# Moving averages of a pooling mixer: running sums on GpSimd, or products with a band matrix on TensorE

## The reference, cut to what matters

```python
csum = pad(cumsum(u, axis=1))                 # per group g of 64 channels
lo   = max(t + 1 - w, 0); cnt = min(t + 1, w)
mean = (csum[:, 1:, g] - csum[:, lo, g]) / cnt
y    = mean - u                               # then y @ w_pool[g], times pool_scale
```

## Time and profile before

| | us |
|---|---|
| median of 3 runs | 1396.54 (1396.28 to 1396.85) |
| the profiled execution | 1395.26 |
| its span | 1393.5 |
| TensorE busy (share of the span) | 1308.9 (94%) |
| VectorE | 727.0 (52%) |
| GpSimd | 562.0 (40%) |
| ScalarE | 476.4 (34%) |

### The profile page before, as it was taken

The page is one execution under the profiler, slowest core; times in us unless marked ns, Lnnn a source line. Parts: engine busy times, 40 slices in busy tenths (PEclk is TensorE's granted clock), DMA queues, the critical chain, the costliest instruction groups (busy, mean ns, idle before and its releaser), DMA issues.

```text
span 1393.5 us, 16477 instructions
## 1 busy us (share of the span) xinstructions
PE 1308.9 (94%) x6506; PEld 1025.5 (74%) x6506; DVE 727.0 (52%) x1045; ACT 476.4 (34%) x948; POOL 562.0 (40%) x312
## 2 busy tenths in 40 slices
PE   7999789997999999999899988989989999999996
PEld 5887555576888888888778855556868888888885
DVE  3154787725876153361464366877169650633506
ACT  4323556822322122221132334577222221312211
POOL 3541840023544444444444429200326444444444
PEclk9999778999999999999989986699989999999998
DMA  7531100022243323232144320000314332333311
GB/s 232 149 91 46 47 1 1 1 81 71 77 135 103 94 92 105 91 104 93 46 128 114 98 60 2 0 1 2 106 46 134 101 98 92 105 91 101 96 61 61
DMA packets 66557, 109.99 MB, mean 79 GB/s; under 512 B 16880, under 2 KB 17200, under 8 KB 66352
## 3 DMA queue, kind: packets, MB, share of 16 engines
q1 hardware_dynamic: 65328, 104.73, 24.4%
q10 hardware_dynamic: 1152, 4.19, 1.0%
HBM read 106.82 MB, written 2.10 MB: 78 GB/s over the span
## 4 chain that ended last, share of the span: by engine, by line
PE 87%; DVE 8%; ACT 2%; POOL 1%; issue 1%; DMA 1%; SPq 0%; POOLq 0%; ACTq 0%; DVEq 0%
PE ps L606 16%; PE ps L607 15%; PE ps L608 15%; PE ps L603 8%; PE ps L605 8%; PE ps L604 8%; PE ps L653 4%; PE ps L661 3%; DVE probs_a L1223 2%; PE ps L697 2%; DVE negmax L1174 1%; PE ps L715 1%; PE ps L682 1%; POOL rstd L494 1%; PE ps L582 1%
## 5 line engine op out<-in xcount | busy, mean ns | idle before, releaser
L480 POOL TENSOR_TENSOR w_lo<-raw,w_hi 128x1024 fp32r<-128x1024 f32 x184 | 452.9, 2466 | 739.5 <-ACT w_hi L857 739.4
L857 ACT ACTIVATE w_hi<-raw 128x1024 fp32r<-128x1024 f32 x184 | 193.9, 1059 | 615.2 <-PE ps L608 398.0
L603 PE MATMUL ps<-xt_hi,w_lo 128*128 128x512 f32 x512 | 202.0, 395 | 4.8 <-DVE xt_lo L1068 4.8
L605 PE MATMUL ps<-xt_lo,w_hi 128*128 128x512 f32 x512 | 200.8, 392 | 0.0
L604 PE MATMUL ps<-xt_hi,w_hi 128*128 128x512 f32 x512 | 200.7, 392 | 0.0
L606 PE MATMUL ps<-w_hi,mt_lo 128*128 128x512 f32 x384 | 150.1, 391 | 0.0
L608 PE MATMUL ps<-w_lo,mt_hi 128*128 128x512 f32 x384 | 149.4, 389 | 0.0
L607 PE MATMUL ps<-w_hi,mt_hi 128*128 128x512 f32 x384 | 149.4, 389 | 0.0
L606 PE MATMUL ps<-w_hi,xt_lo 128*128 128x512 f32 x320 | 127.7, 399 | 4.5 <-DVE xt_lo L1068 3.7
L608 PE MATMUL ps<-w_lo,xt_hi 128*128 128x512 f32 x320 | 126.3, 395 | 0.0
L607 PE MATMUL ps<-w_hi,xt_hi 128*128 128x512 f32 x320 | 126.3, 395 | 0.0
(11 more groups left out here) (174 smaller groups left out, 1974.8 us busy)
## 6 DMA issues: line engine op xcount, KB each, us to landing
raw<-in_w_up SPq DMA_DIRECT2D x64, 512.0 KB, 3.7
raw<-in_w_down SPq DMA_DIRECT2D x64, 512.0 KB, 3.6
raw<-in_w_in SPq DMA_DIRECT2D x40, 512.0 KB, 3.7
raw<-in_w_out SPq DMA_DIRECT2D x8, 512.0 KB, 3.6
raw<-in_w_out SPq DMA_DIRECT2D x12, 256.0 KB, 3.8
xres<-in_x SPq DMA_DIRECT2D x4, 512.0 KB, 6.0
rows<-in_ln_g ACTq DMA_DIRECT2D x4, 512.0 KB, 4.1
rows<-in_ln_b ACTq DMA_DIRECT2D x4, 512.0 KB, 5.8
```

What stands on the lines that cost most here:

```text
L480: nc.gpsimd.tensor_tensor(w_lo[:, u % RING], raw[:, u % RING], w_hi[:, u % RING].bitcast(F32), ALU.subtract).then_inc(s_lo_ready, 1)
L603: mm(o, wl[:, c], a_hi[:, k, :], start=first, stop=False)
L605: return mm(o, wh[:, c], a_lo[:, k, :], start=False, stop=end)
L857: A(w_hi[:, u % RING], raw[:, u % RING], ACT.Copy).then_inc(s_hi_ready, 1)
```

## The change

The means are taken by products on the values as they lie in `proj_b`, tokens on the partitions. The output of `matmul(o, of, band)` is `of` transposed times `band`: the 128 tokens of a tile against a band of 144 columns (128 tokens of the same tile and 16 of the next), with 1/w inside the window and 1 subtracted at the token itself. So one step sums, divides, subtracts and turns. For the first tile the band's first 128 columns are another matrix, with the true counts. The products of the four tiles add up in bank 7, 64 channels of a group in each half of the partitions. GpSimd's sums, their buffers (`upad`, `boxb`, `boxc`), the table of 1/count and the semaphore `s_pool_y` go; the constants get the bands; `boxed` takes the result, and `cst` moves to the space behind it.

```diff
-SIDE = {0: ("turn", 6), 1: ("turn", 12), 2: ("turn", 7), 3: ("turn", 8), 4: ("turn", 9), ...
+SIDE = {0: ("turn", 6), 1: ("turn", 12), 2: ("box", 0), 3: ("box", 1), 4: ("turn", 9), ...
...
+    q = np.arange(BAND)                       # BAND = P + 16
+    for g, w in enumerate(WINDOWS):
+        inside = (q[None, :] >= p[:, None]) & (q[None, :] - p[:, None] < w)
+        here = q[None, :] == p[:, None]
+        k[:, K_BAND + g * BAND:K_BAND + (g + 1) * BAND] = inside / np.float32(w) - here
+        k[:, K_FIRST + g * P:K_FIRST + (g + 1) * P] = (inside / np.minimum(q + 1, w).astype(np.float32) - here)[:, 0:P]
...
-        cst = sb("cst", [4, TT * 6])
+        cst = at("cst", ra + 28672, [4, TT * 6])
...
-                pool.wait_ge(s_side_emptied, nth("side_emptied", layer, 4))
-                nc.gpsimd.memset(upad[:, :, 0:16], 0.0)
...
-                for c in range(2):
-                    b, u_ = boxb[:, c, :], upad[:, c, :]
-                    add = nc.gpsimd.tensor_tensor
-                    link(add(b[:, w], u_[:, w], u_[:, back(1)], ALU.add))
...
-                    add(b[:, w], b[:, w], u_[:, w], ALU.subtract).then_inc(s_pool_y, 1)
...
+                elif kind == "box":
+                    for tt in range(TT):
+                        for g in (2 * c, 2 * c + 1):
+                            r, u0 = 64 * (g % 2), T_U - T_VCM + 64 * g
+                            o, of = ps[r:r + 64, 7, :], proj_b[:, tt, u0:u0 + 64]
+                            band = kc[:, K_BAND + g * BAND:K_BAND + (g + 1) * BAND]
+                            if tt == 0:
+                                mm(o[:, 0:P], of, kc[:, K_FIRST + g * P:K_FIRST + (g + 1) * P], start=True, stop=False,
+                                   skip_group_check=True)
+                                last = mm(o[:, P:BAND], of, band[:, P:BAND], start=False, stop=False, skip_group_check=True)
+                            else:
+                                n = BAND if tt < TT - 1 else P
+                                last = mm(o[:, tt * P:tt * P + n], of, band[:, 0:n], start=False, stop=tt == TT - 1,
+                                          skip_group_check=True)
                 elif kind == "pool":
-                    pe.wait_ge(s_pool_y, nth("pool_y", layer, c + 1))
-                    last = mm(ps[:, 7, :], w_blk[:, c, :], boxb[:, c, 16:16 + SEQ], start=True, stop=True)
+                    last = mm(ps[:, 7, :], w_blk[:, c, :], boxed[:, c, :], start=True, stop=True)
...
-                        last = A(upad[:, c - Q_U, 16:16 + SEQ], b, ACT.Copy)
+                    elif kind == "box":
+                        last = A(boxed[:, c, :], b, ACT.Copy)
```

More of the change, by code:

```diff
@@ L66 @@
 TASKS = 2 * TASKS_A
-SIDE = {0: ("turn", 6), 1: ("turn", 12), 2: ("turn", 7), 3: ("turn", 8), 4: ("turn", 9), 5: ("compress", 0),
+SIDE = {0: ("turn", 6), 1: ("turn", 12), 2: ("box", 0), 3: ("box", 1), 4: ("turn", 9), 5: ("compress", 0),
         6: ("turn", 10), 7: ("turn", 11), 8: ("turn", 13), 9: ("turn", 14), 10: ("cmp_scores", 0),
@@ L78 @@
 R_CAQ, R_SAQ, R_CAK, R_SAK, R_CCK, R_SCK, R_CCQ, R_SCQ = 0, 16, 48, 64, 96, 128, 192, 224
-K_INV = K_ROPE + TT * ROPE_W
-K_CM = K_INV + 2 * SEQ
+BAND = P + 16
+K_BAND = K_ROPE + TT * ROPE_W
+K_FIRST = K_BAND + 4 * BAND
+K_CM = K_FIRST + 4 * P
 K_CB = K_CM + TT * 32
@@ L83 @@
 K_HALF = K_LAM + 2 * DEPTH
-K_ROWS = K_HALF + 1
-K_END = K_ROWS + 6
+K_END = K_HALF + 1
 K_MASK = K_END
@@ L105, in shape_constants @@
     rope = np.concatenate([ca * A_SCALE, sa * A_SCALE, ca, sa, cc, sc, cc * C_SCALE, sc * C_SCALE], -1)
-    k[:, K_ROPE:K_INV] = rope.reshape(P, -1)
-    tt = np.arange(SEQ)
-    for c in range(2):
-        for half in range(2):
-            cnt = np.minimum(tt + 1, WINDOWS[2 * c + half])
-            k[64 * half:64 * half + 64, K_INV + c * SEQ:K_INV + (c + 1) * SEQ] = 1.0 / cnt
+    k[:, K_ROPE:K_BAND] = rope.reshape(P, -1)
+    q = np.arange(BAND)
[4 more added lines that the diff above has]
+        k[:, K_FIRST + g * P:K_FIRST + (g + 1) * P] = (inside / np.minimum(q + 1, w).astype(np.float32) - here)[:, 0:P]
     n = np.arange(32)
@@ L120, in shape_constants @@
     k[:, K_HALF] = -0.5
-    k[:, K_ROWS:K_ROWS + 4] = (p[:, None] // 32 == np.arange(4))
-    k[:, K_ROWS + 4:K_ROWS + 6] = (p[:, None] // 64 == np.arange(2))
     return k
@@ L159 @@
     cmp_rows=1, cmp_max=1, cmp_shifted=1, cmp_factor=1, cmp_exp=1, cmp_probs=1,
-    pool_y=2, pool_hi=2, pool_mixed=2,
+    pool_hi=2, pool_mixed=2,
     scores=TASKS, negmax=TASKS, exped=TASKS, probs=TASKS, p_turned=TURNS, p_copied=TURNS,
@@ L201, in build @@
         xt_hi, xt_lo = at("xt_hi", ra, [KT, SEQ], F32R), at("xt_lo", ra + 16384, [KT, SEQ], F32R)
-        qkt, upad = at("qkt", ra, [S_N, SEQ]), at("upad", ra + 2048 * S_N, [2, 16 + SEQ])
-        boxc = at("boxc", ra + 28800, [16 + SEQ])
+        qkt, boxed = at("qkt", ra, [S_N, SEQ]), at("boxed", ra + 2048 * S_N, [2, SEQ])
         rb = room(32768)
@@ L209, in build @@
         probs_a, pt_a = at("probs_a", rb + 10368, [3, 2, SEQ]), at("pt_a", rb + 22656, [2, 2, SEQ])
-        boxb = at("boxb", rb + 3 * 2048, [2, 16 + SEQ])
         rc = room(32768)
@@ L320, in build @@
         s_value_weights = sem("value_weights")
-        s_pool_y = sem("pool_y")
         s_pool_hi = sem("pool_hi")
@@ L937, in side @@
                     n, (kind, c) = SIDE_NUMBER[t], SIDE[t]
-                    if kind not in ("turn", "compress", "cmp_turn"):
+                    if kind not in ("turn", "box", "compress", "cmp_turn"):
                         return
@@ L951, in side @@
                         last = A(cmp_pt[0:64, 2 * c:2 * c + 2, 1, :], src[0:64, :, 1, :], ACT.Copy)
-                    elif Q_U <= c < Q_QC:
-                        last = A(upad[:, c - Q_U, 16:16 + SEQ], b, ACT.Copy)
+                    elif kind == "box":
+                        last = A(boxed[:, c, :], b, ACT.Copy)
                     else:
```

## The result

The changed kernel takes 1373.72 us (median of 4 runs, 1371.85 to 1376.60) where the kernel before took 1396.41 in the same measurement (1394.55 to 1396.85): a ratio of 0.9842, interval 0.9819 to 0.9865. In four later sets of runs, each on one chip, the kernel before was timed 18, 13, 17 and 7 times; it spread from 1382 to 1398 us, in groups near 1383, 1388, 1390, 1395 and 1397. In the two of these sets that have the changed kernel as well, its ratios were 0.9859 (0.9827 to 0.9890) and 0.9909 (0.9882 to 0.9935). So the gain is 0.9 to 1.6%, and how much of it one sees depends on the kernel before.

What follows compares the result with a forecast made beforehand. GpSimd's sums were taken to block VectorE, which starves TensorE and lowers its clock in the two token-mixer stages. -8.9 - 7.0 + 6.0 = -9.9 us gave 1386.5 us from 1396.54; range 1379 to 1394 us.

Steps and rivals of the forecast that it cites:

- Term A: Task 7 of each layer's token-mixer stage: VectorE's stall behind GpSimd's sums goes, -8.9 us for both layers.
- Term B: TensorE in tasks 7 to 12: the clock stays high for most of the stretch, -3.5 us a layer, -7.0 us.
- what is won stays won: Behind the token-mixer stage: TensorE's chain, next weights already loaded, keeps the gain; no size of its own.
- Term C: Slots 2 and 3 of each layer: band products replacing four turns add 1.5 us each on TensorE's path, +6.0 us.
- Rival 1: Token-mixer stages: denser products in slots 2 and 3 bring the clock up sooner; -16.9 us, 1379.6 us, chance 0.22.
- Rivals 2: Behind task 7: the clock falls anyway, so nothing is gained from it; -2.5 us, 1394.0 us, chance 0.15.
- rival 3: Slots 2 and 3: the band products' weight loads don't overlap products; +10.3 us, 1406.8 us, chance 0.06.
- 4 (another cause): Task 7: something else blocks VectorE and the stall stays; +6.0 us, 1402.5 us, chance 0.03.
- What costs nothing: ScalarE's copies, slots 8, 19 and 20, and the constants' DMA: no wait added, nothing late, no time charged.

Runs made afterwards that it cites:

- box and sums: Changed kernel with GpSimd's twelve elementwise instructions a layer put back, results unused: 1390.83 us, ratio 1.0002 to the kernel before.
- filled gap in the kernel before: Kernel before, sums untouched, with six unused 512-column products ahead of task 7's turn: 1391.37 us, ratio 0.9978.
- without box: Kernel before with GpSimd's sums left out and nothing in their place, means missing from the output: 1378.85 us, ratio 0.9912; again 1378.02 us, ratio 0.9924.
- by halves: Changed kernel with the band products' two loops exchanged, all of one 64-channel half first, then the other: 1373.25 us, ratio 0.9887.

## Why the prediction was wrong

The direction was right, and so was the mechanism of the gain: GpSimd blocks VectorE, VectorE starves TensorE, the starved TensorE loses its clock. The size was wrong by a factor of 2.3 against the median, 1.9 in the profiled executions. The terms as measured there are -8.9 (A), -10.9 (B) and -3.2 us up to task 8, less 4.2 us that the rest of the two stages gives back. That last one had no term: "what is won stays won" was said of the time behind the stage, and the clock between task 12 and the stage's end was put at nothing. (The sum's last step has a slip of 0.1 us: 1396.54 - 9.9 is 1386.6.)

**Term A was right.** Forecast -8.9 us; the maxima of tasks 8 and 9 have come closer by 4.9 and 4.0 us. The experiment with box and sums brings the 5.42 us back.

**Term B was mis-sized.** The step said a gain of 4.5 us a layer if the clock holds, taken at 3.5 for the chance that it falls: -7.0 us. It measured 5.4 and 5.5 us: -10.9. With box and without sums the clock held through this stretch in both layers of every profile, and for the stretch that I put at 7.6 us (6.5 and waits) TensorE took 6.7 us, from 175.76 to 182.48 us in layer 0. The filled gap in the kernel before shows, in one layer of one profile, that it isn't the clock alone: 3.2 us of it are the clock's, the rest needs the unblocked VectorE. And without box the clock did not hold: in three of four stages it fell at 33 us, and tasks 9 to 12 took 9.4 to 9.5 us instead of 7.8. So a part of B depends on C, which the sum kept apart.

**Term C is the step that failed.** Forecast +6.0 us, 1.5 us for each of four boxes: "TensorE is the chain, its groups adjoining, so all of it is on the path". The price of a box was right, even a little high (2.11 and 1.20 us against 2.47 and 1.33; the turns that it replaces 0.9 and 0.5). Two things were not.

The low clock in slots 2 and 3 "in both layers", on which 1.5 us a box stood, was that of one execution. In every profile with box the clock was up 12 to 16 us into the stage, so at most the first box of a layer met the low clock, and the boxes add 1.2 and 0.7 us to the slots, 1.9 us a layer and not 3.0. That box brings the rise forward is not shown: the kernels with turns and no sums rise at 16 us too, the kernel before at 12 (once), 20 (twice) and 29 us (three times, all in layer 1). How much of this is chance, and why layer 1 of the kernel before rose at 29 us each time, stays open.

And what the boxes add did not stay on the path. Against the kernel without box, whose clock rises at the same place, 1.3 to 1.5 us a layer are left at task 7's maximum and nothing at task 12's, because TensorE then waits less for task 7's weighting (0.72 us against 1.27 to 1.62) and keeps its clock there. In task 5 too a wait for VectorE takes up added work (by halves: 1.1 us more in the slots, 0.3 us more at task 8). Measured up to task 8 in the profiled executions: 0.0 and -3.2 us, the -3.2 in layer 1, where the clock rose at 16 instead of 29 us; over the timed runs with box and sums -3.5 to +4.0 us.

Rival 1 (-16.9 us, chance 0.22) has the number nearest to what happened; the profiled executions differ by -18.7. Its cause, denser products that bring the clock forward, is not what the runs show: turns alone had the same rise.

**The range failed** for what the sum started from. I took one execution's clock as the kernel's own. The three runs shown agreed within 0.6 us, and the same program later spread over 15 us. In the two later sets with both kernels the gain was 1.4% and 0.9%, the second inside the range as a ratio (0.9909 is 1383.8 us from 1396.5).

Rivals 2 (clock falls anyway), 3 (bare weight loads) and 4 (another cause) did not happen in the changed kernel. For rival 3: 20 loads and 20 products fit in 1.20 us, 0.06 us a record, so loads overlap products of the same rows here, and the rule of the Trainium skill (TensorE: Matmul & The Clock Gate, Part 3) on row groups is not borne out by this case. What costs nothing was right: slots 8, 19 and 20 wait for nothing new, and the time from the last maximum of layer 0 to the first of layer 1 is 551.4 us against 550.9.

## What to carry to other kernels

An engine on no chain can set the time of one that is: look at the same instruction's duration with the idle engine busy and idle (5.41 against 1.41 us), before asking what the move costs. Work that was moved to a TensorE stage that waits for others did not cost its duration here (1.9 us a layer in the slots, nothing at task 12); ask what it hides behind and what the clock does after it. And where a stage's clock moves within an execution, take a second and a third profile of the kernel before before building a sum on one.

## What the runs showed of the hardware that was not expected

- With the same program the granted clock of a stage rose 12 or 20 us after the start of layer 0's stage, 29 us after layer 1's, and the execution's time came in steps of some us (kernel before: 1383, 1388, 1390, 1395, 1397). The mean granted clock follows only in part: 0.955 near 1383 and 1388 us, 0.949 to 0.951 near 1390 and 0.949 near 1395, 0.943 to 0.948 from 1396 us up. That the place of the rise makes the steps is not shown: the profiles with a rise at 12 and at 20 us took 1396.3 and 1395.3 us.
- Four GpSimd instructions of 1.04 to 1.32 us stretched four VectorE instructions of 0.35 us to 5.4 us in all, about one GpSimd instruction for each. In one of the later profiles of the kernel before the same group began 1.7 us ahead of the sums, not 1.1 us behind their start, and took 3.09 us.
- Products on the two halves of the output partitions are quicker when they alternate: 1.20 us for a box, 1.83 us when one half follows the other.
- Unused products in a gap kept the clock at 2.4 GHz over it (windows at 234 us), at no cost where they ended inside the gap: 6.2 us from task 25's to task 26's maximum with and without them. Behind the gap they cost 2.7 us a layer.
